# One-hots of an expert key: one broadcast comparison, or eight comparisons with a column

## The reference, cut to what matters

```
q = (xb @ w_q).reshape(n, 8, 2, 128)             # 8 heads, two half queries
s = einsum('nhpc,pkc->nhpk', q, sk)              # scores against 128 + 128 sub-keys
sv, si = top_k(s, 16)
cand    = sv[:, :, 0, :, None] + sv[:, :, 1, None, :]
cand_id = si[:, :, 0, :, None] * 128 + si[:, :, 1, None, :]
fv, fi  = top_k(cand, 16)                        # 16 experts for each token and head
eid = take(cand_id, fi);  gw = softmax(fv)
act  = gelu(einsum('nhkd,nd->nhk', u_tab[eid], xb))
y    = einsum('nhk,nhkd->nd', gw * act, v_tab[eid])
```

## Time and profile before

| | |
|---|---|
| median of 3 runs | 3491.95 us (3485.2 to 3493.96) |
| the profiled execution | 3497.0 us, of which the span of instructions is 3495.3 us |
| mean granted TensorE clock | 0.961 |
| TensorE busy | 3239.5 us (93%), weight loads 2780.3 us (80%) |
| VectorE busy | 2078.9 us (59%), 3709 instructions |
| ScalarE busy | 1234.2 us (35%) |
| the spread stages | 1697.7 to about 1844 us, and the same again about 1,068 us later |

### The profile page before, as it was taken

How to read it: one execution, slowest core, us unless ns; L and a number is a source line. 1 busy time by engine, 2 the same in 40 slices (tenths; PEclk the granted TensorE clock), 3 DMA queues, 4 the chain that set the end, 5 groups by cost and what they waited for, 6 DMA issues and landing times.

```text
span 3495.3 us, 52926 instructions
## 1 busy us (share of the span) xinstructions
PE 3239.5 (93%) x20456; PEld 2780.3 (80%) x20456; DVE 2078.9 (59%) x3709; ACT 1234.2 (35%) x1842; POOL 111.7 (3%) x135
## 2 busy tenths in 40 slices
PE   6998998999988999688899999999889899999998
PEld 2566996996767979478899999887668799999986
DVE  2453554554345550439996666685438997666686
ACT  1132433432124431122454444433322354444433
POOL 0100000000000000003100000000002200000000
PEclk8999998999999999699999999999889999999999
DMA  7403554555213534024466665674224466665674
GB/s 274 170 1 118 184 186 170 185 186 197 87 37 132 184 135 152 2 97 142 166 226 228 209 219 205 224 240 145 93 70 146 143 228 245 204 217 211 205 245 138
DMA packets 190525, 580.71 MB, mean 166 GB/s; under 512 B 16768, under 2 KB 61824, under 8 KB 185504
## 3 DMA queue, kind: packets, MB, share of 16 engines
q1 hardware_dynamic: 185120, 541.04, 44.8%
q10 hardware_dynamic: 4608, 33.56, 2.3%
q0 software_dynamic: 640, 4.00, 0.3%
HBM read 543.92 MB, written 34.60 MB: 166 GB/s over the span
## 4 chain that ended last, share of the span: by engine, by line
PE 84%; DVE 11%; ACT 3%; DMA 1%; issue 1%; DVEq 0%; ACTq 0%; SPq 0%; POOL 0%; POOLq 0%
PE ps L926 29%; PE ps L967 25%; PE ps L917 4%; PE ps L803 4%; PE ps L761 4%; PE ps L1168 3%; PE ps L898 2%; PE ps L870 2%; PE ps L806 2%; PE ps L886 2%; DVE w_split L2056 1%; PE ps L955 1%; PE ps L949 1%; DVE arena L1670 1%; PE ps L1133 1%; DVE arena L2079 1%
## 5 line engine op out<-in xcount | busy, mean ns | idle before, releaser
L926 PE MATMUL ps<-x_split,w_split 128*128 128x256 f32 x9312 | 1188.2, 286 | 71.6 <-DVE w_split L2056 41.1
L926 PEld LDWEIGHTS ps<-x_split,w_split 128*128 128x128 f32 x9312 | 1163.1, 193 | 96.6 <-issue 75.7
L967 PE MATMUL ps<-w_split,h_split 128*128 128x512 f32 x3864 | 915.7, 391 | 2.5 <-DVE w_split L2056 2.5
L967 PEld LDWEIGHTS ps<-w_split,h_split 128*128 128x128 f32 x3864 | 713.8, 188 | 143.8 <-issue 2.9
L2056 DVE TENSOR_TENSOR w_split<-ring,w_split 128x1024 fp32r<-128x1024 f32 x512 | 627.9, 1227 | 324.7 <-ACT w_split L1517 323.8
L1517 ACT ACTIVATE w_split<-ring 128x1024 fp32r<-128x1024 f32 x512 | 541.2, 1058 | 387.3 <-PE ps L967 350.8
L1868 DVE TENSOR_TENSOR w_split<-ring,w_split 128x1024 fp32r<-128x1024 f32 x198 | 242.3, 1226 | 237.0 <-ACT w_split L1482 237.0
L1482 ACT ACTIVATE w_split<-ring 128x1024 fp32r<-128x1024 f32 x198 | 209.0, 1059 | 329.6 <-PE ps L926 226.6
L1525 ACT ACTIVATE arena<-ps 128x256 f32<-128x256 f32 (+1 forms) x256 | 98.6, 385 | 460.3 <-PE ps L926 460.3
L917 PE MATMUL ps<-arena,ring 128*128 128x256 f32 (+1 forms) x672 | 152.6, 391 | 9.3 <-DVEq L1664 7.1
L803 PE MATMUL ps<-arena,ring 128*128 128x512 f32 (+1 forms) x416 | 154.1, 525 | 4.8 <-ACTq L1274 4.8
(11 more groups left out here) (262 smaller groups left out, 2555.2 us busy)
## 6 DMA issues: line engine op xcount, KB each, us to landing
ring<-in_peer_u SPq DMA_DIRECT2D x256, 512.0 KB, 3.3
ring<-in_peer_v SPq DMA_DIRECT2D x256, 512.0 KB, 4.2
ring<-in_ffn_in SPq DMA_DIRECT2D x132, 512.0 KB, 3.2
ring<-in_ada SPq DMA_DIRECT2D x96, 512.0 KB, 4.5
ring<-in_ffn_out SPq DMA_DIRECT2D x66, 512.0 KB, 3.2
spread_rows<-arena ACTq DMA_DIRECT2D x32, 1024.0 KB, 4.1
arena<-spread_rows SPq DMA_DIRECT2D x20, 1536.0 KB, 8.4
ring<-in_pq SPq DMA_DIRECT2D x32, 512.0 KB, 3.2
```

The lines of the kernel that those rows point to most:

```text
L926: last = mm(dst, w_split[:, w, wp, at:at + P], rhs[rp], start=(first and i == 0), stop=(final and i == 2), skip_group_check=shared)
L967: last = mm(ps[:, 2 * r + c, :], h_split[:, ph, hp, r * P:(r + 1) * P], w_split[:, b[3], wp, c * 512:(c + 1) * 512], start=(first and i == ...
```

## The change

The comparison for `hot_i` is done token by token: instead of one TENSOR_TENSOR whose second operand is the broadcast key, eight TENSOR_SCALAR instructions, each of which compares `key_row` (128 bf16 numbers) with one column of `chosen`, the f32 copy of the first key. The output tile and its layout are the same, and so are all waits.

```
-                    v.tensor_tensor(hot_i[:, b], over(key_row, GROUP),
-                                    keys[:, 0, at].unsqueeze(2).to_broadcast([P, GROUP, KEYS]), ALU.is_equal)
+                    for u in range(GROUP):
+                        token = s * GROUP + u
+                        v.tensor_scalar(hot_i[:, b, u, :], key_row, chosen[:, 0, token:token + 1], None, ALU.is_equal)
```

## The result

The changed kernel takes 3506.09 us (median of 8 runs, 3504.07 to 3510.95), against 3493.99 us before, now also with 8 runs. The ratio is 1.0037, 95% interval 1.0026 to 1.0048: 12 us slower, measurably. The forecast was 26 us slower, 3518 us; so the sign and the place were right, and the size was twice what came.

What follows compares the result with a forecast made beforehand. The prediction took VectorE, without slack in the spread, as the bound: +0.41 us a step over 64 steps is +26 us, so 3491.95 + 26 = 3518 us, range 3483 to 3526.

Steps and rivals of the forecast that it cites:

- The bound: In the spread VectorE has no slack at 4.54 us a step, and what lies behind does not absorb a delay.
- TensorE's floor: In the spread TensorE waits about 0.08 us a step for the one-hots, so it needs 4.46 us a step.
- The hold of a column instruction: Each new TENSOR_SCALAR in the spread holds VectorE 0.193 us, eight 1.54 us against 1.13, +0.41 us a step.
- the point at which it turns: In the spread, a column instruction must hold VectorE less than 0.14 us for the kernel not to lose.
- the bound from L1766: Upper case in the spread: 0.206 us per column instruction from L1766's median, eight 1.65 us, +0.52 us a step.
- one element a cycle: Main case: the spread's column instructions process one element a cycle, +26 us in all; chance 0.55.
- The case that the prediction named as its own refutation: 16-bit data keep a faster rate in the spread's comparison in spite of the column; the forecast is then 31 us wrong.
- its two main cases: Whole-kernel times: 3486 or so for the faster rates in the spread, 3514 to 3526 for one element a cycle.
- Four elements a cycle: Rival: the spread's column instructions hold 0.11 us each, TensorE decides, 3486 us in all; chance 0.07.
- Two a cycle: Rival: 16-bit data stay paired in the spread, VectorE needs 4.45 us a step, 3487 us in all; chance 0.31.
- A wait of each for the end of the last one: Rival: the spread's small instructions do not overlap, +1.05 us a step, 3559 us; chance 0.05 with other losses.
- the marks: Mean duration of the new instructions: near 0.275 us shows one element a cycle, 0.21 two, 0.17 to 0.18 four.

Runs made afterwards that it cites:

- the constant: The changed kernel with a constant of the instruction in place of the column of `chosen`: 3486.94 us (one run).
- the bf16 column: The changed kernel with the column taken from the bf16 copy of the key in place of the f32 one: 3506.12 us.
- the widths: The changed kernel with sixteen column instructions of 64 elements (3580.03 us), or one of 1,024 (3487.35 us), in place of eight of 128.

## Why the prediction was right in its sign and wrong in its size

**The bound.** Right. VectorE had no slack in the spread, every tenth of a microsecond of it became one of the step, and nothing behind the spread took it back. The runs make a ladder of what the column instructions of a step hold in all and what the kernel takes more than before: 1.08 us gives 0, 1.30 gives 12, 1.56 gives 29, 1.78 gives 40, 2.33 gives 84.

**TensorE's floor.** It was put at 4.46 us a step and is 4.43. The prediction counted only TensorE's wait between L926 and L1168, 0.08 us. Another 0.03 lay inside L1168, whose 24 matmuls took 1.51 us from start to start in the step of the earlier trace rows and take 1.48 when the one-hots are ready (1803.24 to 1804.72 with the constant). The limit of gain is 7 us, not 5.

**The hold of a column instruction** is the step that failed: 0.193 us was taken, 0.163 measured, so +0.17 us a step in place of +0.41, and 11 us in place of 26. The sign held because the point at which it turns, 0.14 us, lay below both. A small misreading beside it changed nothing: in the earlier trace rows an instruction starts 0.08 to 0.10 us before the written end of the one before, not 0.08 throughout, so that the bound from L1766 was 0.19 to 0.20 us and not 0.206.

**Luck.** The choice on which the forecast stood, one element a cycle, was false. Its 0.193 us were some 0.13 for the data and 0.06 for the rest; the runs have 0.033 and 0.130. An error of 0.10 too much and one of 0.07 too little left 0.03. With the first put right alone, the forecast would have been a gain; that its sign came out right is owed to the second. The case that the prediction named as its own refutation, 16-bit data keeping a faster rate in spite of the column, did come, and was to put it wrong by 31 us and by that cause alone; it was 12 us off (3506 against 3518), since the columns cost what the rate gave back. The measured time lies between its two main cases, 3486 and 3514 to 3526, where it had named none.

**What misled.** The prediction drew a slope in f32 from 128 elements (L1766, mostly one column) to 256 (L2005, L2249, two columns) and read it as one element a cycle. The runs show two things mixed there: at two a cycle the 128 more elements cost 0.067 us, and the second column 0.061. The sum, 0.128, looks just like one element a cycle. It then read the longer duration against L1924 (no column) as a lost rate; that too was two columns at 0.061 each (0.122 of 0.403 - 0.281 = 0.122). The trace of the kernel before had the rows that tell the two apart. Its timeline at one step of attention:

```profile
955.48 0.29 DVE L1766 TENSOR_SCALAR arena<-consts,cols 128x128 f32<-128x128 f32 x1
955.68 0.34 DVE L1766 TENSOR_SCALAR arena<-consts,cols,neg_lam 128x128 f32<-128x128 f32 x1
955.94 1.22 DVE L1755 TENSOR_REDUCE cols<-ps 128x2 f32<-128x1024 f32 x1
```

The same line, the same shape: 0.20 us from start to start with one column, 0.26 with two. The prediction mentioned both kinds and did not compare them.

**The rule that was set aside.** The prediction said that this trace contradicts the fp32 part of the Trainium skill, VectorE: DVE Perf Modes, "The perf-mode tier table". It doesn't: with the columns paid for separately, every row of the table above has the rates of that page, four elements a cycle for bf16 and two for fp32, with a column too. The 0.061 us of each column come on top. The Trainium skill, DVE: scalar operands, raw-bit mode, write accounting and state across instructions, "Scalar operands", says a bf16 scale costs the same as an fp32 one; the bf16 column agrees, 0.163 us both.

**The rivals.** Four elements a cycle, with 0.07 the least likely of the three rates, is the true one. But its price was wrong: 0.11 us was put together from instructions without a column, which is what the constant measured (0.101). So the right rate did not bring the gain that was booked for it: 0.061 x 8 = 0.49 us of columns a step turned 0.3 us won into 0.17 lost. Two a cycle is excluded by the widths. A wait of each for the end of the last one is excluded by the hold: 0.163 us from start to start, with 0.251 us of duration.

**The signs to look for.** The mean of the new group was to decide between rates; at 0.251 it matched none of the marks, and a wrong fixed part was not among the cases. The two spreads were to be 13 us longer each; from first to last step they are 145.9 - 140.8 = 5 us longer. TensorE's wait for the one-hots was to show as 0.4 us in every step, and shows in each of the 32, as 0.31 in the mean.

## What to carry to other kernels

Count the columns of the rows from which you take a TENSOR_SCALAR's price: here each cost 0.06 us whatever the width, which on 128 bf16 elements is nearly twice the data's own time. Splitting one broadcast comparison into n column instructions pays only if n times the whole hold is below the hold of the one; here eight times 0.163 against 1.13. If a TENSOR_TENSOR is slow because an operand has a step of 0 in its innermost place, store that operand in pairs: it took the hold from 1.13 to 0.60 us without touching the output's layout. A layout that suits VectorE has to be priced on TensorE too: with the tokens innermost the same 0.60 us came with 359 us more in all.

## What the runs showed of the hardware that was not expected

- A scalar column of VectorE cost 0.061 us of the engine's time per column and instruction (0.101, 0.163 and 0.223 us with none, one and two), for f32 and bf16 columns alike, and left the rate at 0.26 ns an element on bf16 and 0.52 on f32.
- A TENSOR_TENSOR on bf16 ran two elements a cycle over innermost rows of two elements, with the broadcast outside them (0.60 us for 1,024, as against 1.13 with a step of 0 innermost). The Trainium skill, Vector Engine (DVE) Microarchitecture Reference, section "5.1 Performance modes — why throughput varies by op and dtype", gives two 16-bit elements a cycle where the innermost dimension of every operand has a step of 1 and more than one element; the two runs agree.
- TensorE reading its moving operand of 128 bf16 columns with a step of 8 elements took 0.227 us a matmul against 0.061 with the dense operand, as much at a granted clock of 1.00 as at a mean of 0.75. The other operand, hot_w, is read with a step of 8 in both kernels. Behind the first 24 of these matmuls the granted clock fell to 0.50, and over the stage it was 0.67 in the mean, which slowed the other matmuls (24 of L926 in 4.79 us against 2.95).
